# Second mixer: the halves of the mLSTM pieces are dealt to other beats

## The chip, the cores and the metric

The kernel runs on one core of one Trainium2 chip. The metric is the time of one execution on the device, in microseconds. It is one long program for five engines: TensorE (PE), VectorE (DVE), ScalarE (ACT), GpSimd (POOL) and SyncE (SP). They run side by side, and semaphores hold one back until another has done its part.

## What is computed

Two transformer blocks over 512 tokens of width 1024, in float32. The change touches the mixer of the second block alone, which is in short:

```
z = rms_norm(x) @ w_in                 # 1024 -> q, k, v, o of four mLSTM heads (128 wide), gates, and q, k, v of the attention
hm = mlstm(mq, mk, mv, gates)          # four heads
m_out = rms_norm(hm) * sigmoid(mo)
a_out = nsa(aq, ...)                   # compressed, selected and windowed attention, eight heads
x = x + concat(m_out, a_out) @ w_out
```

The mq, mk, mv and mo of the four heads are 16 tiles of 128 x 512. Each is a product of 1024 x 128 weights with the 1024 x 512 input, and the change is about when TensorE makes these products.

## The kernel before

Every product is made in three float32r passes (high by high, high by low, low by high). So the weights come as pieces of 128 x 512: SP loads one into `raw`, ACT writes its high part (`wh`, line 429 in `split_high`), DVE the rest (`wl`, line 441 in `split_low`), and PE multiplies. There are four pairs of `wh` and `wl`. A pair is used again when PE is through with the piece that had it, so the split of a piece waits for the end of the piece four before it.

The mixer is a list of beats, numbered here as in the code by b. In beat b the program does step after step of several things: the scores of attention unit b (PE lines 1800 or 1803), the sums over the values of unit b - 3 (lines 1822, 1830), the transposes of unit b - 2 (line 1851; ACT and DVE copy them out in lines 1883 and 1977), a step of an mLSTM head (`lane`, lines 1996 to 2038), and a run of halves of mLSTM pieces (lines 2137 to 2139, `multiply_m`). `RUN[b]` says how many halves beat b has. A half is six matmuls of 128 x 512, and a piece t is two halves. All engines walk through the same beats, each in its own order of steps, `PE_MIX` for PE and `MIX` for the others.

Two consecutive pieces, t even and t odd, make one tile: PE adds both up in one bank of PSUM. When the odd one is done, DVE takes the tile out of the bank (the take, lines 2425 and 2428, step `mtake`), and the even piece of the next tile writes to the same bank. So its first matmul waits for the take:

```
elif t % 2 == 0 and half == 0:
    e.wait_ge(s_mev, 1 if t == 4 else t // 2)
```

On DVE and ACT a beat's splits stand before its copies, and on DVE the take stands behind both:

```
MIX += run + [("copy", b)]
...
MIX += [("turn", b)]
...
MIX += [("mtake", t // 2) for _, t, half in run if t % 2 and half]
```

On PE the run stands near the end of the beat, before the lane's step:

```
PE_MIX += [("unit", b)] + spread_now + [("sums", b), ("turn0", b), ("turn", b)] + last_sum + run + step
```

Of the kernel before, what the change touches and what calls it, by code (L numbers as in the profile page):

```python
# [53 lines left out]
def build(nc, A, out):  # L54
    with ExitStack() as ctx:
# [1628 lines left out]
            MIX += [("take", 2)] * (k == 7)  # L1684
            MIX += [("z2", k)] + [("cmp", k)] * (1 <= k <= 6) + [("gates", 3 + k // 2)] * (k in (0, 2))

        RUN = [3] * 4 + [2, 2, 4, 2, 2] + [2, 2, 4, 2, 2, 4] * 2 + [2, 2, 2, 2]
        assert sum(RUN) == 64 and len(RUN) == NU - 1
        HALVES = [("m", t, half) for t in range(32) for half in range(2)]
        LANE = 4  # L1690
# [4 lines left out]
        for b in range(NU + 3):  # L1695
            o = sum(RUN[:b])
            run = HALVES[o:o + RUN[b]] if b < len(RUN) else []
            h, s = LANES.get(b, (3, 6) if b == NU + 2 else (-1, -1))
# [1194 lines left out]
```

## Time and profile before

| | us |
|---|---|
| median of 3 runs | 1550.71 (1550.46 to 1550.94) |
| the profiled execution's own time | 1551.23 |
| span in its trace | 1549.5 |
| PE busy | 1529.9 (99%) |
| DVE busy | 988.0 (64%) |
| ACT busy | 709.8 (46%) |
| POOL busy | 173.0 (11%) |

The profiled execution took 0.52 us more than the median. The span is from its first to its last instruction, 1.7 us less than its own time. The beats of this mixer lie between 992 and 1178 us of the span; beat 8 begins at 1039.3 and beat 24 at 1158.7.

### The profile page before, as it was taken

To read this page: it belongs to the slowest core of one execution; us is meant where nothing else is said; L and a number is where in the kernel's file an instruction comes from. 1 tells how busy PE (TensorE), PEld (TensorE's weight loads), DVE (VectorE), ACT (ScalarE), POOL (GpSimd) and SP (SyncE) were. 2 spreads that over 40 slices of the span, in tenths; PEclk is the share of its full clock that TensorE was granted. 3 is DMA by queue.
4 is the path that set the end of the run, shared out by engine and by line. 5 is a ranking of instruction groups with operands and counts; after the bars stand their busy time and mean duration, and the time that the engine had idled before them with its cause. 6 is when DMAs were issued, how large, how long until landed. Compare 5 with 4: busy or idle time off the path is not lost.

```text
span 1549.5 us, 20676 instructions
## 1 busy us (share of the span) xinstructions
PE 1529.9 (99%) x7771; PEld 1258.6 (81%) x7771; DVE 988.0 (64%) x1778; ACT 709.8 (46%) x1420; POOL 173.0 (11%) x159
## 2 busy tenths in 40 slices
PE   8999999999999999999999999999999999999998
PEld 7888888888876798888888887877777888888888
DVE  7876677643788587666672458576766555554367
ACT  7544444333557555444442335355544443433254
POOL 1221222100003202112220000000000010110000
PEclk9999999999999999999999999999999999999999
DMA  6333333334151123333333325321111323333332
GB/s 215 90 101 96 102 96 98 100 102 143 50 164 36 49 69 108 90 101 97 101 95 96 118 70 186 82 62 42 48 42 62 96 96 97 99 97 96 97 114 69
DMA packets 91980, 146.00 MB, mean 94 GB/s; under 512 B 9060, under 2 KB 30948, under 8 KB 91752
## 3 DMA queue, kind: packets, MB, share of 16 engines
q1 hardware_dynamic: 89392, 138.84, 29.7%
q10 hardware_dynamic: 2488, 5.83, 1.2%
q8 instruction: 62, 1.02, 0.3%
q14 instruction: 38, 0.31, 0.1%
HBM read 139.91 MB, written 2.10 MB: 92 GB/s over the span
## 4 chain that ended last, share of the span: by engine, by line
PE 92%; DVE 5%; issue 1%; DMA 1%; ACT 1%; SPq 0%; POOL 0%; DVEq 0%; POOLq 0%; ACTq 0%
PE ps L467 24%; PE ps L469 24%; PE ps L468 24%; PE ps L2137 2%; PE ps L2138 2%; PE ps L2139 2%; PE ps L506 1%; PE ps L507 1%; PE ps L508 1%; PE ps L1851 1%; PE ps L1830 1%; PE ps L1800 1%; DVE X L857 1%; DVE Hl L624 1%; PE ps L1427 1%
## 5 line engine op out<-in xcount | busy, mean ns | idle before, releaser
L441 DVE TENSOR_TENSOR wl<-raw,wh 128x512 fp32r<-128x512 f32 (+2 forms) x417 | 301.3, 727 | 383.2 <-ACT wh L429 382.8
L429 ACT ACTIVATE wh<-raw 128x512 fp32r<-128x512 f32 (+2 forms) x417 | 259.4, 627 | 569.4 <-PE ps L469 531.8
L467 PE MATMUL ps<-Hh,wh 128*128 128x512 f32 x1074 | 420.5, 391 | 1.0 <-DVE st L1925 1.0
L469 PE MATMUL ps<-Hh,wl 128*128 128x512 f32 x1074 | 418.1, 389 | 0.0
L468 PE MATMUL ps<-Hl,wh 128*128 128x512 f32 x1074 | 417.9, 389 | 0.0
L467 PEld LDWEIGHTS ps<-Hh,wh 128*128 128x128 f32 x1074 | 201.6, 188 | 44.0 <-issue 2.4
L469 PEld LDWEIGHTS ps<-Hh,wl 128*128 128x128 f32 x1074 | 201.6, 188 | 42.3
L468 PEld LDWEIGHTS ps<-Hl,wh 128*128 128x128 f32 x1074 | 201.7, 188 | 41.3
L467 PE MATMUL ps<-AH,wh 128*128 128x512 f32 x408 | 158.7, 389 | 0.0
L468 PE MATMUL ps<-AL,wh 128*128 128x512 f32 x408 | 158.7, 389 | 0.0
L469 PE MATMUL ps<-AH,wl 128*128 128x512 f32 x408 | 158.7, 389 | 0.0
L1144 DVE SCALAR_TENSOR_TENSOR t_all<-t_all,cols 128x512 f32<-128x512 f32 x208 | 143.0, 748 | 0.0
L1159 POOL TENSOR_TENSOR t_all<-t_all 128x512 f32<-128x512 f32 x44 | 89.1, 2042 | 370.4 <-ACT t_all L1123 357.6
L468 PEld LDWEIGHTS ps<-AL,wh 128*128 128x128 f32 x408 | 76.6, 188 | 16.0
L467 PEld LDWEIGHTS ps<-AH,wh 128*128 128x128 f32 x408 | 76.6, 188 | 15.8
L469 PEld LDWEIGHTS ps<-AH,wl 128*128 128x128 f32 x408 | 76.6, 188 | 15.8
L1136 DVE TENSOR_TENSOR t_all<-ps,RB 128x512 f32<-128x512 f32 x120 | 74.4, 684 | 8.5 <-ACT RB L536 8.5
L1118 ACT ACTIVATE t_all<-t_all,cols 128x512 f32<-128x512 f32 x104 | 76.4, 802 | 2.0 <-DVE t_all L1136 2.0
L2137 PE MATMUL ps<-Hh,wh 128*128 128x512 f32 x128 | 52.3, 409 | 0.0
L2139 PE MATMUL ps<-Hh,wl 128*128 128x512 f32 x128 | 50.1, 391 | 0.0
L2138 PE MATMUL ps<-Hl,wh 128*128 128x512 f32 x128 | 50.1, 391 | 0.0
L467 PE MATMUL ps<-Hh,xh 128*128 128x512 f32 x113 | 45.5, 403 | 0.2
(378 smaller groups left out, 2200.4 us busy)
## 6 DMA issues: line engine op xcount, KB each, us to landing
raw<-in_w_in SPq DMA_DIRECT2D x216, 256.0 KB, 2.7
raw<-in_w_out SPq DMA_DIRECT2D x104, 256.0 KB, 2.6
raw<-in_w_up SPq DMA_DIRECT2D x64, 256.0 KB, 2.7
raw<-in_w_down SPq DMA_DIRECT2D x32, 256.0 KB, 2.5
raw<-in_w_q SPq DMA_DIRECT2D x16, 256.0 KB, 2.7
raw<-in_w_o SPq DMA_DIRECT2D x16, 256.0 KB, 3.1
raw<-in_w_pg SPq DMA_DIRECT2D x16, 256.0 KB, 2.6
X<-in_xT SPq DMA_DIRECT2D x8, 256.0 KB, 5.4
```

Of the source, the lines that this page charges most:

```text
L429: e.activation(split_in[n][0][:, 0:width], raws[n % NRAW][:, 0:width], ACT.Copy, scale=1.0 if gain is None else gain).then_inc(s_hi, 1)
L441: e.tensor_tensor(wl[:, 0:width], raw, wh[:, 0:width].bitcast(F32), ALU.subtract).then_inc(s_lo, 1)
L467: e.matmul(b, wh[:, o:o + w], xh, start=k == 0, stop=False, skip_group_check=joined)
L468: e.matmul(b, wh[:, o:o + w], xl, start=False, stop=False, skip_group_check=joined)
L469: m = e.matmul(b, wl[:, o:o + w], xh, start=False, stop=k == (nk - HELD - 1 if closing else nk - 1), skip_group_check=joined)
L1118: e.activation(T[4 + i], T[i], ACT.Identity, bias=conv_col(l, g, i, 3), scale=conv_col(l, g, i, 2)).then_inc(s_c2, 1)
L1136: e.tensor_tensor(T[i], L_BANKS[l][4 * (g % 2) + i][:, :], RB[:, :], ALU.mult).then_inc(s_u, 1)
L1144: e.scalar_tensor_tensor(T[4 + i], ts[i][:, tap:TW - 2 + tap], conv_col(l, g, i, tap), T[4 + i], ALU.mult, ALU.add).then_inc(s_to, 1)
L1159: e.tensor_tensor(T[4 + i], T[4 + i], T[6 + i], ALU.mult).then_inc(s_pm, 1)
L2137: e.matmul(b, h, xh, start=t % 2 == 0 and k == 0, stop=False)
L2138: e.matmul(b, h, xl, start=False, stop=False)
L2139: m = e.matmul(b, l, xh, start=False, stop=t % 2 == 1 and k == 3)
```

## The change

One table of numbers:

```
-        RUN = [3] * 4 + [2, 2, 4, 2, 2] + [2, 2, 4, 2, 2, 4] * 2 + [2, 2, 2, 2]
+        RUN = [3] * 4 + [2, 2] + [4, 2, 4, 0, 4, 2, 4, 0, 4, 2, 4, 2, 4, 0, 4, 2, 4, 0, 2]
```

Written out, with the pieces t that each beat multiplies:

| beat | 6 | 7 | 8 | 9 | 10 | 11 | 12 | 13 | 14 | 15 | 16 | 17 | 18 | 19 | 20 | 21 | 22 | 23 | 24 |
|---|---|---|---|---|---|---|---|---|---|---|---|---|---|---|---|---|---|---|---|
| halves before | 4 | 2 | 2 | 2 | 2 | 4 | 2 | 2 | 4 | 2 | 2 | 4 | 2 | 2 | 4 | 2 | 2 | 2 | 2 |
| pieces before | 8, 9 | 10 | 11 | 12 | 13 | 14, 15 | 16 | 17 | 18, 19 | 20 | 21 | 22, 23 | 24 | 25 | 26, 27 | 28 | 29 | 30 | 31 |
| halves now | 4 | 2 | 4 | 0 | 4 | 2 | 4 | 0 | 4 | 2 | 4 | 2 | 4 | 0 | 4 | 2 | 4 | 0 | 2 |
| pieces now | 8, 9 | 10 | 11, 12 | - | 13, 14 | 15 | 16, 17 | - | 18, 19 | 20 | 21, 22 | 23 | 24, 25 | - | 26, 27 | 28 | 29, 30 | - | 31 |

No instruction is added or removed. A piece's splits and the take of its tile move with its halves.

TensorE at beats 8 and 9, before. `wh_64` and `wl_65` hold piece 11, `wh_62` and `wl_63` piece 12; `m_taken_z` is the semaphore of the takes.

```order
4700 L2139 MATMUL ps<-Hh,wl_65 128x512
4701 L2023 MATMUL ps<-b_big 128x128 [waits l_weighted]
4702 L2031 MATMUL ps<-b_mvt,t_all 128x129 [waits l_weighted]
4703 L1800 MATMUL ps<-b_big 128x512 [waits maxima]
4704 L1800 MATMUL ps<-b_big 128x512
4705 L1851 MATMUL ps<-ident,b_Sb_215 128x128 [waits copied_first,scaled]
4706 L1851 MATMUL ps<-ident,b_Sb_215 128x128 x3
4707 L1851 MATMUL ps<-ident,b_Sb_215 128x128 [waits copied_second]
4708 L1851 MATMUL ps<-ident,b_Sb_215 128x128 x3
4709 L2038 MATMUL ps<-b_mvt,t_all 128x129 [waits l_weighted]
4710 L2038 MATMUL ps<-b_mvt,t_all 128x129 x3
4711 L2137 MATMUL ps<-Hh,wh_62 128x512 [waits piece_low,m_taken_z]
```

The same place on TensorE in the changed kernel:

```order
4698 L2137 MATMUL ps<-Hh,wh_64 128x512
4699 L2138 MATMUL ps<-Hl,wh_64 128x512
4700 L2139 MATMUL ps<-Hh,wl_65 128x512
4701 L2137 MATMUL ps<-Hh,wh_62 128x512 [waits piece_low,m_taken_z]
4702 L2138 MATMUL ps<-Hl,wh_62 128x512
4703 L2139 MATMUL ps<-Hh,wl_63 128x512
```

Piece 12 now follows piece 11 at once, and the eleven rows that stood between them come behind it.

VectorE in beat 8, before (line 441 writes the low part of a piece's split, line 1977 is the copy, line 2425 the take of the tile of pieces 10 and 11):

```order
898 L441 TENSOR_TENSOR wl_59<-raw_54,wh_58 128x512 [waits piece_high]
899 L1977 COPY t_all<-ps 128x512 [waits summed,transposed_second]
900 L2425 SCALAR_TENSOR_TENSOR b_big<-ps,RB 128x512 [waits tile_summed]
901 L2093 TENSOR_TENSOR t_all<-ps,t_all 128x128 [waits l_scores,l_decay_masked]
902 L2446 TENSOR_SCALAR b_big<-b_big,cols 128x512 [waits mo_made]
```

VectorE in beat 8 in the changed kernel:

```order
898 L441 TENSOR_TENSOR wl_59<-raw_54,wh_58 128x512 [waits piece_high]
899 L441 TENSOR_TENSOR wl_65<-raw_55,wh_64 128x512 [waits piece_high]
900 L1977 COPY t_all<-ps 128x512 [waits summed,transposed_second]
901 L2425 SCALAR_TENSOR_TENSOR b_big<-ps,RB 128x512 [waits tile_summed]
902 L2093 TENSOR_TENSOR t_all<-ps,t_all 128x128 [waits l_scores,l_decay_masked]
```

The split into `wl_65`, the place of piece 11, moved from beat 9 ahead of the copy and the take of beat 8.

ScalarE in beat 8 in the changed kernel (line 429 writes the high part; lines 1883 and 1888 are its copies):

```order
695 L429 ACTIVATE wh_58<-raw_54 128x512 [waits piece_used,piece_in1]
696 L429 ACTIVATE wh_64<-raw_55 128x512 [waits tile_summed,piece_in2]
697 L1883 ACTIVATE t_all<-ps 128x512 [waits summed,transposed_first]
698 L1888 ACTIVATE b_big<-ps 128x2x128 [waits summed]
```

The split into `wh_64` waits for `tile_summed`, the end of piece 11; before, it stood three rows later, behind the copies and the exponentials of line 1868. The other beats that now have four halves and begin with an odd piece (10, 16 and 22) show the same order on the three engines.

## Rows read from the trace of the kernel before

**Rows 1.** Beats 4 to 24: length, busy (instructions) of PE, PEld, DVE, ACT, POOL, PEclk, DMA.

```profile
1014.00:1166.30 152.30, 151.69 (x859) 108.83 (x857) 107.45 (x320) 78.55 (x236) 7.13 (x17) 1.00 0.19 49
```

**Rows 2.** Waits of PE from 1014 to 1169.5 us: total, times, longest.

```profile
PE ps L467 <- DVE st L1925: 1.0, 1, 1.0
PE ps L2003 <- DVE t_all L2122: 0.5, 1, 0.5
```

**Rows 3.** Timeline of PE, beats 8 to 10: start, length, instruction.

```profile
1046.13 0.39 PE L2139 MATMUL ps<-Hh,wl 128*128 128x512 f32 x1
...
1046.89 1.13 PE L1800 MATMUL ps<-b_big 64*128 64x512 f32 x4
...
1049.69 0.47 PE L2137 MATMUL ps<-Hh,wh 128*128 128x512 f32 x1
...
1052.63 1.14 PE L1803 MATMUL ps<-b_big 64*128 64x256 f32 x8
...
1054.18 1.90 PE L1830 MATMUL ps<-t_all,b_vtok 128*64 128x256 f32 x16
```

**Rows 4.** Timeline of DVE and ACT, beats 8 and 9 (in brackets: idle before, releaser).

```profile
1046.55 0.69 DVE L2425 SCALAR_TENSOR_TENSOR b_big<-ps,RB 128x512 f32<-128x512 f32 x1 [2.05 <-PE ps L2139]
...
1046.61 0.63 ACT L429 ACTIVATE wh<-raw 128x512 fp32r<-128x512 f32 x1 [0.97 <-PE ps L2139]
...
1048.68 0.69 DVE L1925 CUSTOM_DVE_ANT_0 b_Sb<-ps,b_bias 128x512 f32<-128x512 f32 x1
...
1051.09 0.69 DVE L1977 COPY t_all<-ps 128x512 f32<-128x512 f32 x1
```

**Rows 5.** Timeline of beat 6, a run of four halves, at its middle.

```profile
1029.23 0.39 PE L2139 MATMUL ps<-Hh,wl 128*128 128x512 f32 x1
1029.45 0.39 PE L2137 MATMUL ps<-Hh,wh 128*128 128x512 f32 x1
...
1029.71 0.63 ACT L429 ACTIVATE wh<-raw 128x512 fp32r<-128x512 f32 x1 [2.42 <-PE ps L2139]
...
1030.38 0.69 DVE L441 TENSOR_TENSOR wl<-raw,wh 128x512 fp32r<-128x512 f32 x1 [1.04 <-ACT wh L429]
...
1030.99 0.69 DVE L1977 COPY t_all<-ps 128x512 f32<-128x512 f32 x1
```

**Rows 6.** Timeline of PE and DVE, end of beat 16.

```profile
1103.08 0.39 PE L2139 MATMUL ps<-Hh,wl 128*128 128x512 f32 x1
...
1103.83 0.68 DVE L441 TENSOR_TENSOR wl<-raw,wh 128x512 fp32r<-128x512 f32 x1
1103.97 0.66 PE L2003 MATMUL ps<-ident,t_all 128*128 128x128 f32 x4 [0.50 <-DVE t_all L2122]
1104.43 0.55 DVE L1977 COPY t_all<-ps 128x384 f32<-128x384 f32 x1
...
1104.90 0.68 DVE L2428 TENSOR_TENSOR b_big<-ps,RB 128x512 f32<-128x512 f32 x1
```

**Rows 7.** Timeline of DVE in beat 11 and of PE in beat 12.

```profile
1067.65 0.68 DVE L1977 COPY t_all<-ps 128x512 f32<-128x512 f32 x1
...
1070.14 1.95 PE L1830 MATMUL ps<-t_all,b_vtok 128*64 128x256 f32 x16
```

**Rows 8.** Timeline of ACT and PE, beat 23.

```profile
1154.59 0.58 ACT L2044 ACTIVATE t_all<-ps 128x512 f32<-128x512 f32 x1
...
1154.92 0.47 PE L2137 MATMUL ps<-Hh,wh 128*128 128x512 f32 x1
...
1157.77 1.02 PE L2023 MATMUL ps<-b_big 128*128 128x512 f32 x2
```

**Rows 9.** Stretches around the first fall of the granted clock: length, PE busy, PEclk, DMA.

```profile
29.20:32.63 3.43, 2.54 (x22) 1.00 0.27 76
32.63:36.04 3.41, 3.28 (x15) 0.50 0.27 79
```

**Rows 10.** The page's DMA issues: size and median us to landing.

```profile
raw<-in_w_in SPq DMA_DIRECT2D x216, 256.0 KB, 2.7
```

## The prediction

> **What bounds the kernel now.** I read the views in this order: the busy time of the stretch that the change touches, then PE's waits in it, then the timeline of the beats whose runs move. From 1014 to 1166.3 us, which are beats 4 to 24, PE is busy for 151.69 of 152.30 us at the full granted clock (1.00, that is 2.4 GHz), DVE for 107.45 and ACT for 78.55 [rows 1]. PE waits here for two things only, 0.5 us before line 2003 in beat 16, and, behind the last beat, 1.0 us before line 467 [rows 2]. So PE's list of matmuls sets the time. What shortens a list of matmuls that nothing interrupts is little; what opens a wait in it counts in full, since PE is just as full behind the mixer and nothing there takes up a delay.
>
> **What the change does, part by part.**
>
> *1. Runs that begin with an odd piece.* The runs of four halves before all began with an even piece, so that both pieces belonged to one tile. Beats 8, 10, 16 and 22 now multiply 11 and 12, 13 and 14, 21 and 22, 29 and 30. The first piece closes a tile and the second, which starts the next one in the same bank, has to wait for the take. Before, the next beat's scores, sums and transposes lay between the two. In beats 8 and 9 the closing piece's last matmul began at 1046.13, the take at 1046.55, and it lasted 0.69 [rows 3, 4]; piece 12 began at 1049.69 [rows 3], some 2.4 us after the take's end. Now PE would begin piece 12 0.22 us after 1046.13 (the step from one matmul to the next, [rows 5]).
>
> The take itself would keep PE for 0.42 + 0.69 + some 0.04 for the semaphore - 0.22 = 0.93 us, 1.0 with the slower first matmul of a run. That is the lower bound for a wait. But the take doesn't stand first on DVE. The run's second piece brings a second split, and in DVE's order the split and the copy of line 1977 stand ahead of the take. The split needs ACT's high part, and ACT's needs the buffers that piece 11 frees when it ends. So all of it begins only after piece 11's last matmul. The trace of before has this chain, harmless, in the middle of each run of four. In beat 6 [rows 5], counted from the start of the last matmul of the first piece (1029.23): ACT begins the high part at +0.48 (1029.71), DVE the low part at +1.15 (1030.38, it waited for ACT), the copy at +1.76 (1030.99). The take then begins one copy later: a copy of 512 has the same 0.69 as the split, so the same step of 0.61, which makes +2.37. It lasts 0.69 [rows 4], to +3.06, and PE goes on at +3.10. Without a wait it would have gone on at +0.22, so the wait is 2.88 us. The first matmul of a run takes some 0.08 more than a later one: 2.95 us a time. The upper bound is the same chain with DVE late. In beat 16 DVE is late: its first split starts at 1103.83, 0.75 after the closing matmul at 1103.08, because of its work for the lane; from there a second split, the copy of 384 (line 1977 to line 2428: 0.47) and the take (0.68) give 1103.83 + 0.61 + 0.60 + 0.47 + 0.68 + 0.04 = 1106.23 against 1103.30, that is 2.93, or 3.0 with the first matmul [rows 6]. The order lists show the same three rows ahead of the take in all four beats. I take 3 x 2.95 + 3.0 = 11.85 us.
>
> *2. Runs that go away.* Beats 9, 13, 19 and 23 have none. The engine pays a start for each run. Twelve matmuls at 0.226 are 2.71, the run of beat 9 took 1052.63 - 1049.69 = 2.94 [rows 3], others some 0.1 above 2.71. Four starts fewer, one of them of 0.23, are worth -0.45 us.
>
> *3. A wait that gets covered.* In beat 16 PE reached line 2003 at 1103.30 and waited for DVE's line 2122 until 1103.97, 0.67 us [rows 6]. Piece 22 and its wait of 3 us now stand ahead of line 2003: -0.67.
>
> *4. What the empty beats had covered.* An empty beat is 2.7 to 2.9 us shorter for PE, so everything that PE needs at the start of the next one has that much less room. Beat 9 is 1049.69 - 1046.89 = 2.80 long without its run [rows 3]. The scores of unit 9 are processed at 1048.68 + 0.69 = 1049.37, 2.48 after the beat's begin [rows 4]: 0.3 us in hand for line 1803 of beat 10. The sums of beat 10 (line 1830) begin 1.55 after 1052.63, so now 4.35 after the begin of beat 9, and need DVE's copy, which before ended at 1051.09 + 0.69 = 1051.78, 4.89 after it, and now comes one split (0.60) earlier, at 4.29 [rows 3, 4]: a tie, for which I put 0.2. Beat 11 loses two halves and one split: its copy ended at 1068.34, now 0.60 earlier, 1067.74; line 1830 of beat 12 began at 1070.14, now 2.72 earlier, 1067.42 [rows 7]: 0.35. In beat 23 line 2023 would follow the transposes at once, at 1154.92, and needs ACT's line 2044, which ends at 1155.17; with the load of its weights some 0.5 [rows 8]. Sum +1.05. Elsewhere I found at least 0.4 in hand.
>
> *5. Loads.* SP loads a piece as soon as its `raw` is free, five ahead. A load lands after 2.7 us [rows 10] and five pieces are over 13 us of PE's time even in the densest of the new beats, so a split that moves one beat forward finds its data. Nothing.
>
> **The sum.** 11.85 - 0.45 - 0.67 + 1.05 = +11.8 us on the profiled execution's own 1551.23, which makes 1563.0. That execution stands 0.52 above the median of the runs shown, so the prediction is **1562.5 us**.
>
> **Rivals.**
>
> *The clock falls in the waits.* The granted clock fell to 0.50 (1.2 GHz) at 32.63 us, for 3.41 us, after a stretch in which PE was busy for 2.54 of 3.43 us and much of that with products of few columns [rows 9]; in PE's other waits, of a microsecond or less [rows 2], it stayed at 1.00. The four new waits are longer than these. Such a stretch costs half its length, 1.7 us. One fall, which I think about as likely as none, is in my range: 1564.2. Two or more make 1565.9 to 1569.3. For: waits of nearly 3 us have no like in the mixer. Against: PE is full ahead of each wait and behind it. The Trainium skill (TensorE: Matmul & The Clock Gate, "HAM oscillation — how this bites in real kernels") says that waits between bursts of matmuls can bring the clock down so that each burst begins slowly; by that rule all four waits would be followed by such a stretch, 1569.3. The trace agrees as far as one fall at 32.63 us goes.
>
> *The empty beats starve PE by more.* DVE's beat 9 goes on long after PE has left it. If PE had to wait some 0.9 us behind each of the four empty beats instead of the 1.05 in all of part 4, that would be +2.6: 1565.1. Against it is what stands in part 4: the scores are just in time, and the copy loses its split.
>
> *The take alone.* If the second split didn't stand in the take's way (ACT ahead of it, DVE free), a wait would be its lower bound of 1.0: 4 x 1.0 - 0.45 - 0.67 + 1.05 = +3.9, 1554.6. Against: ACT's split can't begin before piece 11 ends, in whatever way the engines stand.
>
> *Not slower.* This takes that the bank is free when the second piece wants it; then parts 2 and 3 remain, -1.1: 1549.6. It decides at 0.22 us after the closing piece's last matmul. The take begins 0.42 after it at the earliest [rows 3, 4], so I give this next to nothing. That the change doesn't do what it says is ruled out by the order lists.
>
> **How the numbers follow.** The four long waits, with at most one fall of the clock: 0.77. Two or more falls: 0.11. Starved: 0.07. The take alone, or something between: 0.04. Not slower: 0.01. The likeliest gives 1562.5. Its own uncertainty is 0.3 in each of the four waits, 1 in the empty beats and one fall of the clock, 1560.3 to 1565. For 8 in 10 the range reaches a bit into the neighbours on both sides, 1559.5 to 1566.5. 0.2% is 3.1 us, about what a measurement of this kernel can tell from no change. Only the last rival is not above it by more: slower 0.97, same 0.02, faster 0.01.
>
> **What would show it.** In the changed kernel's trace PE has four gaps of nearly 3 us before line 2137, ended by line 2425 or 2428, in beats 8, 10, 16 and 22; DVE's row order there is 441, 441, 1977, take without a gap between the second 441 and the take; the wait before line 2003 in beat 16 is gone; the wait before line 467 is still 1.0. The prediction is wrong if the gaps are of 1 us, if there are others of their size behind beats 9, 13, 19 or 23, or if the granted clock leaves 1.00 between 1030 and 1180 us more than once.

## The result, and the profile after

| | before | after |
|---|---|---|
| median of 4 runs, us | 1550.83 (1550.46 to 1550.97) | 1567.66 (1567.50 to 1568.17) |
| the profiled execution's own time | 1551.23 | 1567.5 |
| span in its trace | 1549.5 | 1565.8 |
| PE busy | 1529.9 (99%) | 1535.6 (98%) |

The change makes the kernel slower by 1.1%: the ratio is 1.0111, 95% interval 1.0099 to 1.0123. The prediction was 1562.5 us with a range of 1559.5 to 1566.5. The sign was right; the time is 5.2 us above the forecast and outside the range.

The page of after, its parts 1 and 5. PE's busy time went up by 5.7 us although it has the same 7771 matmuls, and line 2137 has a wait that it did not have:

```profile
PE 1535.6 (98%) x7771; PEld 1262.2 (81%) x7771; DVE 987.8 (63%) x1778; ACT 709.7 (45%) x1420; POOL 173.2 (11%) x159
...
L2137 PE MATMUL ps<-Hh,wh 128*128 128x512 f32 x128 | 54.6, 426 | 10.9 <-DVE b_big L2428 8.2
L2138 PE MATMUL ps<-Hl,wh 128*128 128x512 f32 x128 | 51.7, 404 | 0.0
L2139 PE MATMUL ps<-Hh,wl 128*128 128x512 f32 x128 | 51.6, 403 | 0.0
```

The stretch of after that answers to [rows 1], beats 4 to 24, in the same columns, and under it the slow stretch at the start, which answers to [rows 9]:

```profile
1013.53:1182.24 168.71, 157.37 (x859) 112.33 (x858) 107.23 (x320) 78.32 (x236) 7.20 (x17) 0.97 0.17 44
...
32.36:35.77 3.41, 3.41 (x16) 3.41 (x17) 2.51 (x7) 2.32 (x5) 0.49 (x1) 0.50 0.32 85
```

It was 152.30 us long and is now 168.71: these 16.41 us are the whole difference of the two profiled executions (1567.5 - 1551.23 = 16.27). PE is busy for 5.68 us more in it and its granted clock is 0.97 instead of 1.00, while DVE and ACT work as long as before.

PE's waits in this part of after, 1014 to 1200 us (total, times, longest), which answer to [rows 2]:

```profile
PE ps L2137 <- DVE b_big L2428: 8.2, 3, 2.8
PE ps L2137 <- DVE b_big L2425: 2.7, 1, 2.7
PE ps L467 <- DVE st L1925: 1.0, 1, 1.0
PE ps L1830 <- DVE t_all L1977: 0.4, 1, 0.4
```

So the four waits of the forecast are there, with its size and its releasers; the wait of line 2003 is gone, and one of 0.4 us before line 1830 is new. Together these are some 11 us. The rest is seen only when the matmuls behind the waits are timed. The timeline of after in beat 8, on PE, ACT and DVE:

```profile
1045.66 0.39 PE L2139 MATMUL ps<-Hh,wl 128*128 128x512 f32 x1
1046.15 0.63 ACT L429 ACTIVATE wh<-raw 128x512 fp32r<-128x512 f32 x1 [7.09 <-PE ps L2139]
...
1046.81 0.69 DVE L441 TENSOR_TENSOR wl<-raw,wh 128x512 fp32r<-128x512 f32 x1 [3.69 <-ACT wh L429]
...
1047.42 0.68 DVE L1977 COPY t_all<-ps 128x512 f32<-128x512 f32 x1
...
1048.02 0.68 DVE L2425 SCALAR_TENSOR_TENSOR b_big<-ps,RB 128x512 f32<-128x512 f32 x1
...
1048.76 0.50 PE L2137 MATMUL ps<-Hh,wh 128*128 128x512 f32 x1 [2.71 <-DVE b_big L2425]
1049.09 0.39 PE L2138 MATMUL ps<-Hl,wh 128*128 128x512 f32 x1
...
1049.99 0.63 PE L2138 MATMUL ps<-Hl,wh 128*128 128x512 f32 x1
1050.42 0.63 PE L2139 MATMUL ps<-Hh,wl 128*128 128x512 f32 x1
```

The chain up to 1048.76 is the predicted one, step by step: from the closing matmul at 1045.66 the high split begins at +0.49, the low at +1.15, the copy at +1.76, the take at +2.36, and PE goes on at +3.10. But the matmuls after it do not run as before. From 1049.99 they start 0.43 us apart, against 0.22 to 0.23 at full clock [rows 5]. Four stretches of after, one at or behind each wait: the first, second and fourth are cut where the trace shows the clock change, the third, where it shows no change, to the same length (length, PE, PEld, DVE, ACT, POOL, PEclk, DMA):

```profile
1049.53:1052.94 3.41, 3.41 (x9) 2.65 (x8) 0.00 (x0) 0.00 (x0) 0.00 (x0) 0.50 0.07 21
...
1066.60:1070.01 3.41, 3.35 (x8) 2.68 (x9) 0.00 (x0) 0.00 (x0) 0.00 (x0) 0.50 0.31 79
...
1114.41:1117.80 3.39, 2.46 (x11) 2.04 (x12) 0.88 (x2) 0.00 (x0) 0.00 (x0) 1.00 0.61 160
...
1165.58:1168.99 3.41, 3.04 (x7) 2.46 (x8) 0.32 (x1) 0.00 (x0) 0.00 (x0) 0.50 0.27 77
```

In or shortly behind the waits of beats 8, 10 and 22 the granted clock is at 0.50 (1.2 GHz) for 3.41 us. Behind that of beat 16 it stays at 1.00 (2.4 GHz). Nothing else in the mixer has a stretch at 0.50. The profiled execution is not a special one: the mean granted clock of the four executions of after is 0.992 to 0.994, and that of the kernel before, in all that were run beside the experiments, 0.996 to 0.999.

What each of these costs: a run of 24 matmuls that begins with an even piece takes 5.55 us in this trace. With the 2.95 that the forecast gives a wait it would take 8.50. The run of beat 16 took 8.60, those of beats 8, 10 and 22 took 10.14, 10.13 and 9.96. The clock so cost 1.64, 1.63 and 1.46, together 4.7 us. The stretch of 168.71 us without them is 11.7 us longer than before (16.41 - 4.73).

### The profile page after: what moved, and what is told of

Its sections match the earlier page's. It is cut to its first block, busy times and chain, and to the rows that moved or that the text cites. A ratio compares the mean times of both kernels' runs of the same rounds, so it can differ in the third digit from the quotient of the medians.

```text
span 1565.8 us, 20676 instructions
## 1 busy us (share of the span) xinstructions
PE 1535.6 (98%) x7771; PEld 1262.2 (81%) x7771; DVE 987.8 (63%) x1778; ACT 709.7 (45%) x1420; POOL 173.2 (11%) x159
## 4 chain that ended last, share of the span: by engine, by line
PE 92%; DVE 4%; issue 1%; ACT 1%; DMA 1%; SPq 0%; POOL 0%; DVEq 0%; POOLq 0%; ACTq 0%
PE ps L467 24%; PE ps L468 24%; PE ps L469 24%; PE ps L2137 2%; PE ps L2138 2%; PE ps L2139 2%; PE ps L506 2%; PE ps L508 2%; PE ps L507 2%; PE ps L1830 1%; PE ps L1851 1%; PE ps L1800 1%; PE ps L1427 1%; PE ps L1458 1%; DMA M<-in_x 1%
```

## The experiments

**Theories.** A: the waits cost what was forecast (11.85 us for four), and the clock that falls in them costs the rest; each fall is caused by the wait. B, the rival: the waits alone are dearer than their length, or the empty beats are, and the clock's fall has another cause. The useless matmuls of some runs below write to a bank that nobody reads at that time, so they change nothing in the output. In every diff the minus line is that of the changed kernel unless it says otherwise. The kernel before, run beside them, had a median of 1550.61 us (15 runs) with the first four and 1550.49 (16 runs) with the last four.

**Useless matmuls in the waits** (e1_fill12): PE still waits for the take, but with 12 matmuls in hand.

```
+        FILLED = {12: 8, 14: 10, 22: 16, 30: 22}
...
+                        if t in FILLED:
+                            e.wait_ge(s_sm, FILLED[t] + 1)
+                            for _ in range(12):
+                                e.matmul(turned[4][:, :], Hh[:, 0, 0:P], Hh[:, 0, :], start=True, stop=True)
                         e.wait_ge(s_mev, 1 if t == 4 else t // 2)
```

> The changed kernel, with 12 useless matmuls of 128x512 put into each of the four waits (into the idle bank of the scores, so PE's operands and the order of everything else stay). They take 12 x 0.226 = 2.7 us, which fits into a wait of 2.9 us. Theory (the waits cost 2.95 each and the falls of the granted clock in beats 8, 10 and 22 cost 1.6 each on top): the waits' cost stays, the clock stays at 1.00 in the mixer, and the time falls by 4.8 us against the changed kernel, to 1562.9. Rival (the runs in beats 8, 10 and 22 are longer for another reason, such as late operands, and the clock record only goes along with it): the time stays at 1567.7 or grows.

Measured: 1562.57 us (1562.13 to 1562.85), ratio to before 1.0078 (1.0061 to 1.0094), 5.1 us less than the changed kernel. The timeline of this kernel in beat 8 (the useless matmuls are line 2169, the take line 2431), and under it the same stretch in the columns of [rows 1]:

```profile
1045.04 0.39 PE L2139 MATMUL ps<-Hh,wl 128*128 128x512 f32 x1
1045.27 2.88 PE L2169 MATMUL ps<-Hh 128*128 128x512 f32 x12
...
1047.40 0.68 DVE L2431 SCALAR_TENSOR_TENSOR b_big<-ps,RB 128x512 f32<-128x512 f32 x1
1048.14 0.50 PE L2137 MATMUL ps<-Hh,wh 128*128 128x512 f32 x1
1048.48 0.39 PE L2138 MATMUL ps<-Hl,wh 128*128 128x512 f32 x1
```

```profile
1045.04:1048.14 3.10, 3.10 (x14) 2.26 (x13) 1.89 (x3) 2.61 (x7) 0.00 (x0) 1.00 0.06 5
```

The useful work goes on 3.10 us after the closing matmul, exactly as in the changed kernel. Only the idleness is gone, and with it all three falls of the clock: the trace has none in the mixer, and the mean granted clock of the four executions is 0.997 to 0.998, as in the kernel before. That settles the two terms of the sum: the delay is worth 1562.57 - 1550.61 = 12.0 us (forecast 11.8), the idleness of TensorE another 5.

**The take ahead of the second split** (e2_take_first): on DVE the take of the four tiles moves from behind the copy to just behind the closing piece's own split. The wait remains, short.

```
+        TAKE_FIRST = (11, 13, 21, 29)
...
+                    if what == "m" and k in TAKE_FIRST:
+                        dve_mtake(e, k // 2)
...
+                    if 2 * i[0] + 1 not in TAKE_FIRST:
+                        dve_mtake(e, i[0])
```

(`dve_mtake` holds the take's lines unchanged.)

> The changed kernel, but on DVE the take in beats 8, 10, 16 and 22 stands ahead of the second split instead of behind the split and the copy. Theory (the wait is the chain ACT split, DVE split, copy, take): each wait shrinks from 2.95 to about 1.0 us, no wait is long enough for the clock to fall, and the time is 1550.8 + 4 x 1.0 - 0.45 - 0.67 + 0.9 = 1554.6. Rival 1 (the wait comes from the bank's take alone, not from its place): nothing changes, 1567.7. Rival 2 (the clock falls because of the thinner beats, not because of the long waits): the waits shrink but three falls stay, 1559.4.

Measured: 1555.37 us (1555.05 to 1556.04), ratio 1.0030 (1.0018 to 1.0042). PE's waits for the take from 1014 to 1200 us in this kernel, and its timeline in beat 16:

```profile
PE ps L2137 <- DVE b_big L2383: 3.3, 3, 1.7
...
PE ps L2137 <- DVE b_big L2380: 0.8, 1, 0.8
```

```profile
1104.45 0.39 PE L2139 MATMUL ps<-Hh,wl 128*128 128x512 f32 x1
1104.47 0.56 DVE L2119 TENSOR_TENSOR t_all<-ps,st 128x384 f32<-128x384 f32 x1
...
1105.21 0.68 DVE L441 TENSOR_TENSOR wl<-raw,wh 128x512 fp32r<-128x512 f32 x1
...
1105.81 0.68 DVE L2383 TENSOR_TENSOR b_big<-ps,RB 128x512 f32<-128x512 f32 x1
...
1106.55 0.50 PE L2137 MATMUL ps<-Hh,wh 128*128 128x512 f32 x1 [1.70 <-DVE b_big L2383]
```

Three waits have the lower bound of the forecast (PE idle for 0.78, 1.0 with the restart). In beat 16 it is 1.70, because DVE has its work for the lane ahead of the split and of the take; the expectation had left that out, and these 0.9 us more are as much as the 0.8 us by which it missed. The clock didn't fall in any of the four. So most of the slowdown is the order of three rows on DVE, and what remains is slower than before all the same.

**Runs that begin odd, without empty beats** (e3_odd_full): four runs that begin with an odd piece, in beats 10, 13, 16 and 19.

```
-        RUN = [3] * 4 + [2, 2] + [4, 2, 4, 0, 4, 2, 4, 0, 4, 2, 4, 2, 4, 0, 4, 2, 4, 0, 2]
+        RUN = [3] * 4 + [2, 2] + [4, 2, 2, 2, 4, 2, 2, 4, 2, 2, 4, 2, 2, 4, 2, 2, 2, 2, 2]
```

> Four runs of four halves that begin with an odd piece (beats 10, 13, 16, 19), and no beat without a run: the runs of the kernel before with these four swapped with the run behind them. Theory (the odd begin alone makes the long waits, the empty beats add only some tenths): four waits of 2.95 us in beats 10, 13, 16 and 19, so 1550.8 + 11.8 - 0.67 = 1561.9 if the clock holds, and 1.6 more for each fall, which I expect in two of the four: 1565.2. Rival (the empty beats are what costs): close to 1551.

Measured: 1566.01 us (1564.99 to 1567.66), ratio 1.0100 (1.0085 to 1.0115). The profile has four waits of 2.6 to 2.8 us, and behind three of them the clock at 0.50 for 3.41 us:

```profile
PE ps L2137 <- DVE b_big L2428: 10.8, 4, 2.8
```

```profile
1060.99:1064.40 3.41, 3.41 (x9) 2.63 (x10) 0.00 (x0) 0.00 (x0) 0.00 (x0) 0.50 0.27 73
1088.90:1092.30 3.40, 3.33 (x15) 2.78 (x16) 0.21 (x2) 1.00 (x4) 0.29 (x1) 1.00 0.35 82
1112.19:1115.60 3.41, 3.13 (x7) 2.49 (x8) 0.23 (x1) 0.00 (x0) 0.00 (x0) 0.50 0.52 151
1142.91:1146.32 3.41, 3.41 (x10) 2.64 (x9) 0.00 (x0) 0.34 (x1) 0.00 (x0) 0.50 0.00 0
```

Two falls had been expected, 1565.2 us. The empty beats are not needed for the slowdown. Here the clock fell in beat 16 and stayed up in beat 13. The four runs of this kernel lie 2.7 us apart, those of e1_fill12, without falls, 0.7.

**Empty beats, and every run even** (e4_even): the four empty beats stay, but each run of four begins with an even piece.

```
-        RUN = [3] * 4 + [2, 2] + [4, 2, 4, 0, 4, 2, 4, 0, 4, 2, 4, 2, 4, 0, 4, 2, 4, 0, 2]
+        RUN = [3] * 4 + [2, 2] + [4, 2, 2, 0, 4, 4, 4, 0, 4, 2, 2, 4, 4, 0, 4, 4, 2, 0, 2]
```

> Beats 9, 13, 19 and 23 empty as in the changed kernel, but every run of four halves begins with an even piece (runs of beats 6 to 24: 4 2 2 0 4 4 4 0 4 2 2 4 4 0 4 4 2 0 2). Theory: no wait for a take, no fall of the clock; what stays is -0.4 for four runs fewer and up to +1.0 behind the empty beats: 1550.5 to 1551.5. Rival (empty beats starve PE and let the clock fall): some us above 1551, with gaps behind beats 9, 13, 19 and 23.

Measured: 1550.80 us (1550.07 to 1551.30, 10 runs), ratio 1.0002 (0.9993 to 1.0011). PE's waits are those of before, and no other:

```profile
PE ps L467 <- DVE st L1925: 1.0, 1, 1.0
PE ps L2003 <- DVE t_all L2122: 0.5, 1, 0.5
```

What the empty beats cost in this kernel is lost in the noise: the interval reaches from 1.1 us less to 1.7 us more than before, and part 4 of the prediction, some 1 us, lies within it. Beyond that, the slowdown hangs on the odd beginnings.

**One odd beginning alone** (e5_one_pair): beat 8 as changed, beats 10 and after as before.

```
-        RUN = [3] * 4 + [2, 2] + [4, 2, 4, 0, 4, 2, 4, 0, 4, 2, 4, 2, 4, 0, 4, 2, 4, 0, 2]
+        RUN = [3] * 4 + [2, 2] + [4, 2, 4, 0, 2, 4, 2, 2, 4, 2, 2, 4, 2, 2, 4, 2, 2, 2, 2]
```

> Only beats 8 and 9 are as in the changed kernel (4 and 0 halves), all others as before: one odd begin instead of four. Theory: one wait of 2.95 us, two tenths less for one run fewer, 1550.6 + 2.7 = 1553.3 with the clock at 1.00 and 1554.9 with one fall in beat 8; I expect the fall, since the changed kernel had it there: 1554.9. Rival (what the waits cost is partly given back or added later, beyond the pair): clearly off both numbers.

Measured: 1555.12 us (1554.97 to 1555.80, 5 runs), ratio 1.0031 (1.0019 to 1.0043): 4.6 us for one wait of 2.7. That is one fall more than the 1553.3 us which were worked out for a clock that holds. The profiled execution (1555.77, 0.65 above the median) shows the clock at 0.50 already before PE goes on at 1047.88, and for 6.83 us on end, twice as long as in the changed kernel. Cut here in the middle, PE is busy throughout the second half:

```profile
1047.21:1050.62 3.41, 2.74 (x7) 2.16 (x8) 0.61 (x2) 0.85 (x4) 0.00 (x0) 0.50 0.31 77
1050.62:1054.04 3.42, 3.42 (x11) 2.73 (x9) 0.14 (x1) 0.00 (x0) 0.00 (x0) 0.50 0.00 0
```

**Shorter idleness** (e6_fill2 and e7_fill4): the edit of e1_fill12 with `range(2)` and `range(4)`. PE goes on as late as before, but is idle for 2.25 and 1.80 us instead of 2.7 (in beat 16 for 0.06 more).

> The changed kernel with only 2 useless matmuls at the begin of each long wait, so that PE is idle for about 2.2 us instead of 2.7; the waits end when they did. With all falls of the clock still there 1567.6, with none 1562.6; each one that is left is worth 1.6. I expect one or two left: 1565. If the length of the idle time didn't matter, all three would be left.

> The same with 4 useless matmuls, PE idle for about 1.8 us in each wait: no fall left, 1562.6. If idle time of less than 2 us is enough to bring the clock down, up to 1567.6.

Measured: 1565.07 us (1563.97 to 1565.96), ratio 1.0096 (1.0081 to 1.0111), and 1565.31 us (1563.87 to 1566.81), ratio 1.0096 (1.0082 to 1.0110). The trace of e6_fill2 has one fall, in beat 16. That of e7_fill4 has two, in beats 8 and 16 (its four runs, in the columns of [rows 1]):

```profile
1048.86:1052.27 3.41, 3.41 (x9) 2.63 (x8) 0.00 (x0) 0.00 (x0) 0.00 (x0) 0.50 0.08 23
1065.80:1069.20 3.40, 3.24 (x16) 2.70 (x17) 0.11 (x1) 0.00 (x0) 0.00 (x0) 1.00 0.32 81
1113.71:1117.12 3.41, 3.41 (x10) 2.64 (x9) 0.00 (x0) 0.00 (x0) 0.00 (x0) 0.50 0.27 78
1165.10:1168.50 3.40, 3.20 (x16) 2.66 (x17) 0.14 (x1) 0.00 (x0) 0.00 (x0) 1.00 0.23 77
```

For e6_fill2 I had expected one or two falls and 1565 us, which it had. For e7_fill4 I had expected no fall, and that failed: 1.80 us of idleness is still enough, in some of the waits. The medians of the two kernels can't be told apart. Both are 2.5 to 2.7 us above that of e1_fill12 and 2.4 to 2.6 below that of the changed kernel. The one fall of e6_fill2 is not typical of it: the profiled execution is the fastest of its four (1563.97 us, mean granted clock 0.996), and the other three took 0.9 to 2.0 us more at a mean of 0.994 to 0.995. So the traces don't show that the longer idleness has fewer falls.

**The one gap of before closed** (e8_full16): the kernel before, with the runs of beats 14 to 17 dealt 2, 2, 4, 4, so that four even-begun halves stand ahead of line 2003 in beat 16.

```
-        RUN = [3] * 4 + [2, 2, 4, 2, 2] + [2, 2, 4, 2, 2, 4] * 2 + [2, 2, 2, 2]
+        RUN = [3] * 4 + [2, 2] + [4, 2, 2, 2, 2, 4, 2, 2, 2, 2, 4, 4, 2, 2, 4, 2, 2, 2, 2]
```

(Here the minus line is that of the kernel before.)

> The kernel before with the run of four halves of beat 14 moved to beat 16 (runs of beats 14 to 17: 2 2 4 4), every run of four still beginning with an even piece. The 0.67 us that PE waits in beat 16 for DVE's rows should be covered by the longer run: 1550.6 - 0.6 = 1550.0, hardly to be told from before by its times but to be seen in the trace (the gap before line 2003 gone). If DVE falls behind by what the second split adds, the gap stays and the time is that of before.

Measured: 1549.50 us (1548.76 to 1550.84, 11 runs), ratio 0.9994 (0.9986 to 1.0003). The wait before line 2003 is gone from the trace; the median is 1.0 us below that of before, but the interval holds no change too. Of all versions none is faster than the kernel before by more than the measurement tells.

## Why the prediction was wrong

*1. Runs that begin odd, 11.85 us: right.* From the closing matmul to the next one it took 3.093 us in beats 8, 10 and 22 and 3.156 in beat 16. Less the 0.226 of a step and with some 0.1 for the slower first matmul that is 2.97 each and 3.04, 11.95 in all. That DVE is late in beat 16 was right as well, and that it costs only 0.06 more.

*2 and 3. Starts that go away and line 2003.* In beat 16 line 2003 now follows the last matmul of the run after 0.23 us (0.89 before): -0.66, forecast -0.67. The -0.45 for four starts was not measured by itself. e4_even, which drops the same four, moved by +0.2 us, with an interval of some 1.4 on either side, so it neither shows nor excludes it. In the trace of before the runs of beats 9, 13, 19 and 23 take 2.94, 2.82, 2.85 and 2.85 us, some 0.6 in all above four times 2.71; the term was a little too small, by its own figures too (0.23 and three times 0.08 to 0.1 are 0.47 to 0.53).

*4. Behind the empty beats, 1.05: about right as a sum, partly wrong in place.* Beat 12 waits before line 1830 as forecast (0.39 idle, and 0.46 in the time from line 1800 to it; forecast 0.35):

```profile
1077.96 0.92 PE L1800 MATMUL ps<-b_big 64*128 64x384 f32 x4
1078.43 0.68 DVE L1977 COPY t_all<-ps 128x512 f32<-128x512 f32 x1
1079.27 1.95 PE L1830 MATMUL ps<-t_all,b_vtok 128*64 128x256 f32 x16 [0.39 <-DVE t_all L1977]
```

In beat 10, called a tie, there was none. In beat 23 lines 1851 and 2023 together took 0.41 more (forecast 0.5), and in beat 9 line 2038 took 0.18 more, which wasn't forecast.

The terms give 11.95 - 0.6 - 0.66 + 1.05 = 11.7, the same as the stretch of after without its falls, and e1_fill12, which has all of them and no fall of the clock, measured 12.0.

*The failed step is the rival "The clock falls in the waits", which the sum took at nothing.* Its mechanism and its price for a fall were written down (1.7 us; measured 1.64, 1.63 and 1.46, 4.7 in all). What was wrong is its chance: one fall was thought as likely as none, two or more falls got 0.11, and the sum took none. The argument against it was that PE is full ahead of each wait and behind it. It is, and the clock fell all the same, in three of four. In after, ahead of the fall in beat 8:

```profile
1046.11:1049.53 3.42, 0.78 (x3) 0.67 (x4) 1.89 (x3) 2.79 (x7) 0.00 (x0) 1.00 0.23 56
```

The nearest row for a fall was PE busy for 2.54 of 3.43 us ahead of it [rows 9]; the waits of [rows 2], a microsecond and less, were taken as the other side. A wait of 2.9 us is longer than any of these, so the rows gave no ground for 0.11. They didn't give the number of falls either. Before's own trace has a stretch in which PE did less than in that of [rows 9], at the wait before line 467, and the clock stayed up (length, PE, PEclk, DMA):

```profile
1166.00:1169.40 3.40, 2.41 (x16) 1.00 0.00 0
```

With the three falls the sum would have been 1562.5 + 4.7 = 1567.2.

The Trainium skill (TensorE: Matmul & The Clock Gate, "HAM oscillation — how this bites in real kernels") has the rule that waits between bursts of matmuls can make each burst begin slowly. Its example has waits of some 3 to 5 us, longer than those here, so that 2.7 us are enough is what the traces show and not the page. By the rule I had worked out 1569.3, for all four. The trace agrees with it for beats 8, 10 and 22 and not for beat 16. It was nearer than the forecast.

*What stays open:* which of the waits is followed by a fall. It doesn't hang on the beat: beat 16 stayed at full clock in the changed kernel and fell in e3_odd_full, e6_fill2 and e7_fill4. Nor does it hang strictly on length, since in the profiled executions 1.80 us of idleness had two falls and 2.25 us one. And it isn't fixed by the program. All these kernels have the same instructions until the mixer, and eight of the ten traces have the fall near 33 us of [rows 9]; those of e3_odd_full and e7_fill4 don't. Here is e3_odd_full at that place, in the columns of [rows 9]:

```profile
29.20:32.63 3.43, 2.40 (x20) 1.00 0.32 88
32.63:36.04 3.41, 3.41 (x31) 1.00 0.39 112
```

So the same gap is followed by a fall in one execution and not in another. One trace of each kernel can't tell why.

## What to carry to other kernels

When TensorE is the bound, a wait of it can cost more than its length: ask for each new wait not only how long PE stands idle but what the clock is afterwards, and look for a row with as long an idleness before calling it harmless. A run of accumulations that crosses from one use of a PSUM bank to the next has to wait for the bank's reader, so place the crossing where other matmuls lie between, and look at what stands ahead of that reader in its own queue; here three rows on VectorE made 2.7 us out of 0.8. If such a wait can't be avoided, useless matmuls that fill it can keep the clock at full speed (5.1 us won here with 12 in each of four waits; with 2 or 4 in each some falls stayed), but they give back none of the delay itself.

## What the runs showed of the hardware that was not expected

- Idleness of 2.7 us between two bursts of full-speed matmuls brought the granted clock to 0.50 for 3.41 us in three waits of four (changed kernel), in e3_odd_full, with 2.6 to 2.8 us, also in three of four, and in the one wait of e5_one_pair. In the profiled executions it was one of four at 2.25 us and two of four at 1.80 us; it did not happen at 0.78 us (three waits), nor at the single 1.70 us of e2_take_first.
- At 0.50 the matmuls of 128x512 start 0.43 us apart instead of 0.22 to 0.23.
- The clock can stay down longer: for 6.83 us in e5_one_pair, with PE busy throughout the last 3.42.
- The same instructions can have a fall in one execution and none in another (near 33 us: a fall in eight traces, none in e3_odd_full and e7_fill4).
